# One set-up stage that also norms the memory, and head norms that take their roots of 12 rows

## The reference, cut to what matters

```python
def rms_norm(x, g):
    xf = x.astype(F32)
    y = xf * lax.rsqrt(jnp.mean(xf * xf, axis=-1, keepdims=True) + EPS)
    return (y * g.astype(F32)).astype(x.dtype)

def memory_attention(q_mem, mem, mem_norm_g, w_mem_kv):
    kv = rms_norm(mem, mem_norm_g) @ w_mem_kv
    ...

def diff_attention(q, k, v, lam, lam_init, subln_g):
    ...
    o = o.transpose(1, 0, 2, 3, 4).reshape(B, S, DA_HEADS, 2 * DA_HEAD_DIM)
    o = rms_norm(o, subln_g) * (1.0 - lam_init)
    ...

def hgrn2_mixer(h, mem, w_in, lb, out_norm_g, mem_norm_g, w_mem_kv, w_out):
    ...
    o = hgrn2_chunkwise(heads(q), heads(k), heads(i), heads(log_f))
    o = rms_norm(o, out_norm_g) * jax.nn.silu(heads(g).astype(F32))
    ...
```

## Time and profile before

| | us |
|---|---|
| median of 3 runs (3336.98 to 3337.41) | 3337.23 |
| the profiled execution | 3336.55 |
| its span from first to last instruction | 3334.8 |
| start of the first product of mem_kv | 41.99 |
| subln, from its first square to its last product | 182.18 to 197.83 |
| out_norm_b, likewise | 626.12 to 643.72 |
| first product of out_a, of out_b | 200.66, 646.52 |

### The profile page before, as it was taken

How to read it: one execution, slowest core, us unless ns; L and a number is a source line. 1 busy time by engine, 2 the same in 40 slices (tenths; PEclk the granted TensorE clock), 3 DMA queues, 4 the chain that set the end, 5 groups by cost and what they waited for, 6 DMA issues and landing times. The chain is left out here.

```text
span 3334.8 us, 41604 instructions
## 1 busy us (share of the span) xinstructions
PE 3026.1 (91%) x17165; PEld 2621.3 (79%) x17165; DVE 2031.3 (61%) x2255; ACT 1532.7 (46%) x1743; POOL 27.1 (1%) x47
## 2 busy tenths in 40 slices
PE   5979988679999999989999998999989896987898
PEld 5869876568888889678888887897788795985797
DVE  3547646545545457488898896545556565666645
ACT  3443343234434346367777775433334453432443
POOL 1001000000000000000000000000000000000000
PEclk9989998789999999999999999999999897988999
DMA  4428641034444546479999996533343341434042
GB/s 153 152 79 260 231 153 51 7 151 179 186 168 178 198 180 245 184 295 351 363 356 352 356 366 255 174 118 114 107 150 109 114 151 52 152 128 155 26 166 105
DMA packets 207408, 605.97 MB, mean 182 GB/s; under 512 B 20024, under 2 KB 78166, under 8 KB 163959
## 3 DMA queue, kind: packets, MB, share of 16 engines
q1 hardware_dynamic: 200906, 587.83, 48.5%
q0 software_dynamic: 4064, 12.75, 1.2%
q10 hardware_dynamic: 2253, 2.77, 0.3%
HBM read 602.26 MB, written 1.05 MB: 181 GB/s over the span
## 5 line engine op out<-in xcount | busy, mean ns | idle before, releaser
L1867 DVE TENSOR_TENSOR w_lo<-ring,w_hi 128x2048 fp32r<-128x2048 f32 x336 | 769.5, 2292 | 349.9 <-ACT w_hi L1769 345.0
L1769 ACT ACTIVATE w_hi<-ring 128x2048 fp32r<-128x2048 f32 x336 | 643.0, 1915 | 370.7 <-PE ps L1718 193.2
L344 DVE TENSOR_TENSOR w_lo<-ring,w_hi 128x2048 fp32r<-128x2048 f32 (+2 forms) x228 | 472.4, 2074 | 550.1 <-ACT w_hi L335 549.6
L335 ACT ACTIVATE w_hi<-ring 128x2048 fp32r<-128x2048 f32 (+2 forms) x228 | 396.4, 1739 | 709.7 <-PE ps L446 541.6
L446 PE MATMUL ps<-h_hi,w_hi 128*128 128x256 f32 x1608 | 462.4, 288 | 27.5 <-DVE w_lo L344 15.9
L446 PE MATMUL ps<-h_lo,w_hi 128*128 128x256 f32 x1608 | 459.0, 285 | 0.0
L446 PE MATMUL ps<-h_hi,w_lo 128*128 128x256 f32 x1608 | 458.9, 285 | 0.0
L446 PEld LDWEIGHTS ps<-h_hi,w_hi 128*128 128x128 f32 x1608 | 313.0, 195 | 31.9 <-issue 30.4
L446 PEld LDWEIGHTS ps<-h_lo,w_hi 128*128 128x128 f32 x1608 | 312.9, 195 | 0.2
L446 PEld LDWEIGHTS ps<-h_hi,w_lo 128*128 128x128 f32 x1608 | 312.8, 194 | 0.0
L1694 PE MATMUL ps<-w_hi,h_hi 128*128 128x512 f32 x448 | 179.4, 400 | 4.9 <-DVE w_lo L1867 4.9
(11 more groups left out here) (520 smaller groups left out, 6021.0 us busy)
## 6 DMA issues: line engine op xcount, KB each, us to landing
ring<-in_moe_w_gate_up SPq DMA_DIRECT2D x224, 1024.0 KB, 6.9
ring<-in_moe_w_down SPq DMA_DIRECT2D x112, 1024.0 KB, 6.8
ring<-in_w_in SPq DMA_DIRECT2D x54, 1024.0 KB, 6.9
ring<-in_w_in_even SPq DMA_DIRECT2D x28, 1024.0 KB, 7.0
ring<-in_dense_w_gate_up SPq DMA_DIRECT2D x22, 1024.0 KB, 7.7
ring<-in_w_in_odd SPq DMA_DIRECT2D x16, 1024.0 KB, 6.8
arena<-in_w_ada POOLq DMA_DIRECT2D x24, 512.0 KB, 5.0
ring<-in_w_out_even SPq DMA_DIRECT2D x12, 1024.0 KB, 7.3
```

Source lines behind the costliest of these rows:

```text
L335: k.nc.scalar.activation(self.part(k.w_hi, b, m), src, ACT.Copy).then_inc(k.hi_ready, 1)
L344: k.nc.vector.tensor_tensor(self.part(k.w_lo, b, m), src, self.part(k.w_hi, b, m).bitcast(F32), ALU.subtract).then_inc(k.lo_ready, 1)
L1769: nc.scalar.activation(high(g, h), raw(g, h), ACT.Copy).then_inc(k.hi_ready, 1)
L1867: nc.vector.tensor_tensor(low(g, h), raw(g, h), high(g, h).bitcast(F32), ALU.subtract).then_inc(k.lo_ready, 1)
```

## The change

`mem_norms` is gone as a stage; its work is written into `setup`, and so is the split of the first panel of mem_kv, which that stage then skips. The rows go out on three queues, 13 each (ACT, POOL and SP). SP loads `mem` and the identity first, then its rows, then `x` and the other constants, then the panels. ACT issues the four lambda vectors ahead of its rows. PE waits for rows and identity only. The mean of squares of the memory comes from `bn_stats` and `bn_aggr` on DVE in place of the sums on ACT. ACT and DVE hand over chunk by chunk, not in pairs.

subln and out_norm_b use a new function. Its 12 sums (6 heads by 2 tiles of tokens) are each put on a partition of their own by a matmul with a stationary operand of 12 columns, one of which is 1/128. Root and inverse are taken once, of 12x128 values. Twelve matmuls with a selecting operand then spread the inverses over 128 partitions in PSUM.

```diff
     def open_stage(self, prepare):
 
+        if self.at == 0:
+            return
         prepare(self.place(self.jobs[self.at][0], 0, 0), (1,) if self.begins_early(self.at) else (0, 1))
...
+def head_norm(k, name, x, gain, tmp, gate=None):
...
+        @st.block.scalar
+        def _(act):
+            nc.scalar.activation(k.stat[:, 0:1], k.eps(1e-6), ACT.Sqrt)
+            for p in range(pairs):
+                nc.scalar.activation(flat(tmp, p), flat(x, p), ACT.Square).then_inc(squared, 1)
+            act.wait_ge(sums_ready, 1)
+            nc.scalar.activation(root, k.ps[0:rows, 6, 0:P], ACT.Sqrt, bias=k.eps_cols[0:rows, 0:1]).then_inc(root_ready, 1)
+
+        @st.block.tensor
+        def _(pe):
+            pe.wait_ge(pick_ready, 1)
+            for h in range(HEADS1):
+                pe.wait_ge(squared, h // 2 + 1)
+                for t in range(TT):
+                    r = TT * h + t
+                    last = nc.tensor.matmul(k.ps[0:rows, 6, 0:P], pick[:, rows - 1 - r:2 * rows - 1 - r],
+                                            tmp[:, h, t * P:(t + 1) * P], start=(r == 0), stop=(r == rows - 1))
+            last.then_inc(sums_ready, 1)
+            pe.wait_ge(spread_ready, 1)
+            pe.wait_ge(scale_ready, 1)
+            for p in range(pairs):
+                for i in range(2 * TT):
+                    last = nc.tensor.matmul(k.ps[:, p, i * P:(i + 1) * P], spread[:, 2 * TT * p + i, :], root,
+                                            start=True, stop=True)
+                last.then_inc(scale_spread, 1)
+
+        @st.block.vector
+        def _(dve):
+            o = Order(dve, dve_order)
+            o(nc.vector.memset(pick, 0.0))
+            nc.vector.memset(pick[:, rows - 1:rows], 1.0 / P).then_inc(pick_ready, 1)
+            nc.vector.tensor_copy(spread, k.ident[0:rows, 0:rows].unsqueeze(2).broadcast_to([rows, rows, P])
+                                  ).then_inc(spread_ready, 1)
+            if gate is not None:
+                for p in range(pairs):
+                    dve.wait_ge(squared, p + 1)
+                    nc.vector.scalar_tensor_tensor(flat(x, p), flat(x, p), gain, flat(gate, p), ALU.mult,
+                                                   ALU.mult).then_inc(gated, 1)
+            dve.wait_ge(root_ready, 1)
+            nc.vector.reciprocal(root, root).then_inc(scale_ready, 1)
+            for p in range(pairs):
+                dve.wait_ge(scale_spread, p + 1)
+                if gate is not None:
+                    dve.wait_ge(gated, p + 1)
+                    nc.vector.tensor_tensor(flat(x, p), flat(x, p), k.ps[:, p, :], ALU.mult)
+                else:
+                    nc.vector.scalar_tensor_tensor(flat(x, p), flat(x, p), gain, k.ps[:, p, :], ALU.mult, ALU.mult)
...
         @st.block.sync
         def _(sp):
+            sp.dma_start(v.mem_tok, w["mem"].rearrange("(t p) d -> p t d", p=P)).then_inc(mem_loaded, 16)
+            sp.dma_start(k.ident[:, :], c["ident"]).then_inc(ident_loaded, 16)
+            sp.wait_ge(zeroed, 1)
+            for dst, src in pieces[2::3]:
+                sp.dma_start(dst, src).then_inc(rows_by_sp, 16)
             sp.dma_start(k.x[:, :, :], w["x"].rearrange("(t p) d -> p t d", p=P)).then_inc(loaded, 16)
-            sp.dma_start(v.mem_tok, w["mem"].rearrange("(t p) d -> p t d", p=P)).then_inc(loaded, 16)
             for dst, name in small:
                 sp.dma_start(dst[:, :], c[name]).then_inc(loaded, 16)
             k.stream.load_range(sp, 0, SLOTS)
...
         @st.block.scalar
         def _(act):
-            act.wait_ge(zeroed, 1)
-            for dst, src in pieces[0::2]:
-                act.dma_start(dst, src).then_inc(rows_loaded, 16)
             for i, name in enumerate(("a_lam_q1", "a_lam_k1", "a_lam_q2", "a_lam_k2")):
                 act.dma_start(lam[:, i, :], w[name].flatten().partition_broadcast(P)).then_inc(lam_loaded, 16)
+            act.wait_ge(zeroed, 1)
+            for dst, src in pieces[0::3]:
+                act.dma_start(dst, src).then_inc(rows_loaded, 16)
             act.wait_ge(lam_sums, 1)
             nc.scalar.activation(k.small[:, 2:4], k.small[:, 0:2], ACT.Exp).then_inc(lam_exps, 1)
+            act.wait_ge(mean_ready, 1)
+            nc.scalar.activation(k.stat[:, 4:6], k.stat[:, 2:4], ACT.Sqrt).then_inc(root_ready, 1)
+            act.wait_ge(columns_ready, 1)
+            for c in range(DC):
+                act.wait_ge(mem_turned, c + 1)
+                nc.scalar.activation(high_a[:, c, :], chunk(c), ACT.Identity, scale=gain_a(c)).then_inc(mem_high, 1)
+                nc.scalar.activation(high_b[:, c, :], chunk(c), ACT.Identity, scale=gain_b(c)).then_inc(mem_high, 1)
+            k.stream.round_weights(act, first_panel)
...
         @st.block.tensor
         def _(pe):
-            pe.wait_ge(rows_loaded, 16 * len(pieces[0::2]))
-            pe.wait_ge(more_rows_loaded, 16 * len(pieces[1::2]))
-            pe.wait_ge(loaded, 16 * (2 + len(small)))
+            pe.wait_ge(ident_loaded, 16)
+            pe.wait_ge(rows_by_sp, 16 * len(pieces[2::3]))
+            pe.wait_ge(rows_loaded, 16 * len(pieces[0::3]))
+            pe.wait_ge(more_rows_loaded, 16 * len(pieces[1::3]))
...
+            pe.wait_ge(mem_scaled, TT)
+            for c in range(DC):
+                if c == 6:
+                    pe.wait_ge(columns_ready, 1)
+                for t in range(TT):
+                    last = nc.tensor.transpose(chunk(c)[:, t * P:(t + 1) * P], k.xn[:, t, c * P:(c + 1) * P],
+                                               k.ident[:, :])
+                last.then_inc(mem_turned, 1)
...
         @st.block.vector
         def _(dve):
...
+            dve.wait_ge(mem_loaded, 16)
+            for t in range(TT):
+                for half in range(2):
+                    o(nc.vector.bn_stats(k.half_stats[:, t, half, :], v.mem_tok[:, t, half * 512:(half + 1) * 512]))
...
+            for c in range(DC):
+                dve.wait_ge(mem_high, 2 * c + 2)
+                nc.vector.scalar_tensor_tensor(low_a[:, c, :], chunk(c), gain_a(c), high_a[:, c, :].bitcast(F32),
+                                               ALU.mult, ALU.subtract)
+                nc.vector.scalar_tensor_tensor(low_b[:, c, :], chunk(c), gain_b(c), high_b[:, c, :].bitcast(F32),
+                                               ALU.mult, ALU.subtract)
+            k.stream.rest_of_weights(dve, first_panel)
```

More of the change, by code:

```diff
@@ L1017, in _ @@
                     nc.vector.tensor_tensor(of(out, p), of(tmp, p), of(gate, p), ALU.mult)
+def head_norm(k, name, x, gain, tmp, gate=None):
+    nc = k.nc
+    rows = HEADS1 * TT
+    pick = k.norm_row[:, 0:2 * rows - 1]
+    spread = k.norm_row[0:rows, P:P + rows * P].rearrange("p (r n) -> p r n", r=rows)
+    root = k.norm_row[0:rows, P + rows * P:2 * P + rows * P]
+    flat = lambda y, p: y[:, 2 * p:2 * p + 2, :].rearrange("p h n -> p (h n)")
+    pairs = HEADS1 // 2
+    with stage(k, name) as st:
+        dve_order, pick_ready, spread_ready = st.sem("dve_order"), st.sem("pick_ready"), st.sem("spread_ready")
+        squared, sums_ready, root_ready = st.sem("squared"), st.sem("sums_ready"), st.sem("root_ready")
+        scale_ready, scale_spread, gated = st.sem("scale_ready"), st.sem("scale_spread"), st.sem("gated")
+        @st.block.scalar
[43 more added lines that the diff above has]
+                    nc.vector.scalar_tensor_tensor(flat(x, p), flat(x, p), gain, k.ps[:, p, :], ALU.mult, ALU.mult)
@@ L2100, in setup @@
     nc = k.nc
-    small = [(k.ident, "ident"), (k.ones, "ones"), (k.upper, "upper"), (k.causal, "causal"),
+    small = [(k.ones, "ones"), (k.upper, "upper"), (k.causal, "causal"),
              (k.pair_rot, "pair_rot"), (k.half_rot, "half_rot"), (k.freq, "freq"), (k.cmp_mask, "cmp_mask"),
@@ L2142, in _ @@
             pool.wait_ge(zeroed, 1)
-            for dst, src in pieces[1::2]:
+            for dst, src in pieces[1::3]:
                 pool.dma_start(dst, src).then_inc(more_rows_loaded, 16)
@@ L2168, in _ @@
             nc.vector.memset(k.small[:, 4:5], 0.0).then_inc(lam_sums, 1)
+            dve.wait_ge(mem_loaded, 16)
+            for t in range(TT):
+                for half in range(2):
+                    o(nc.vector.bn_stats(k.half_stats[:, t, half, :], v.mem_tok[:, t, half * 512:(half + 1) * 512]))
+            for t in range(TT):
+                o(nc.vector.bn_aggr(k.moments[:, t, :], k.half_stats[:, t, :, :].rearrange("p h n -> p (h n)")))
+            mean, variance = k.moments[:, :, 0], k.moments[:, :, 1]
+            o(nc.vector.tensor_tensor(mean, mean, mean, ALU.mult))
+            nc.vector.scalar_tensor_tensor(k.stat[:, 2:4], mean, 1e-6, variance, ALU.add, ALU.add).then_inc(mean_ready, 1)
             dve.wait_ge(lam_exps, 1)
@@ L2375, in block1 @@
     attention(k, "diff_attention", groups + memory_groups(k, v.qm, v.km[0], v.vm[0], v.cat), v.work)
-    head_pairs = [((h, h + 2), WHOLE) for h in range(0, HEADS1, 2)]
```

(6 more changed lines are left out.)

43 lines of the change are left out of this document (28 added, 15 removed).

## The result

The changed kernel takes 3316.72 us (median of 4 executions, 3311.57 to 3319.36) against 3337.11 for the kernel before; the ratio is 0.9939, 95% interval 0.9927 to 0.9951. That is 20.4 us or 0.61% faster, clear of the 0.2%. The forecast was 3307.8 in a range of 3300.5 to 3314: right in direction, wrong in size by 9 us, and outside its range. The profiled execution took 3318.24 us, 18.3 less than that of before, where 29.4 were forecast.

What follows compares the result with a forecast made beforehand. PE was busy 91% of the span, but set-up (a DMA, PE, DVE, ACT chain) and two DVE-bound norms lay outside its cover. 14.9 + 14.5 = 29.4 us off 3336.55 gave 3307.2, with 0.7 for the median 3307.8; range 3300.5 to 3314.

Steps and rivals of the forecast that it cites:

- PE does four matmuls of 128 columns after each ... the first four spreading matmuls take 0.65 or 1.1: Norms: PE's sums after each square end at 3.9 us warm, 4.9 cold; first four spreading matmuls 0.65 or 1.1 us.
- the warm figure was 3.9: Norms: with PE at full clock the sums are there 3.9 us into the stage; cold, 4.9.
- The terms of 9.9 and 9.8 us: Cold lengths of the new norms: subln 15.65 - 9.9 = 5.7 us saved, out_norm_b 17.60 - 9.8 = 7.8.
- the 14.5 us of the two stages: Saving taken for subln and out_norm_b together, between 13.5 us cold and 16.7 warm.
- the cold transposes: Set-up's sixteen transposes in 3.30 us, read as PE's lower-clock pitch of 0.19 to 0.21 us a product.
- 1.16 for eight: Norms: eight matmuls in 1.16 us, read as a full-clock pitch of about 0.13 us for 128 columns.
- sums that may still be warm: Norms: the first sums of the squares may still meet the full clock, so 14.5 us saved was taken, cold being 13.5.
- The forecast of 8.3 warm: Norms: at full clock DVE paces the three last products and the stage ends at 8.3 us; cold, 9.9.
- Set-up: 14.9 forecast: First product of mem_kv moves from 41.99 to 27.1 us, saving 14.9; bounds 11.5 to 16.5.
- The lambda loads ... I take 8.0: Set-up: lambda loads, issued by ACT ahead of its rows, land by 7.5 to 11.6 us; 8.0 taken.
- The panel's wait: Rival: panels issued later become the wait; loss over 0.2% chance 0.02, milder delay eating set-up's gain (3322.7) 0.04.
- All later stages should keep their lengths: Sign to look for: stages behind the changed ones stay as long as before; wrong if one grows by what was won.

Runs made afterwards that it cites:

- one_record: The changed kernel with selecting operand and inverses as fp32r, so each spreading product rounds its inputs and is one record; 3309.34 us.
- squares_first: The changed kernel with one line moved: the root that only loads ACT's table comes behind the three squares in the norms; 3308.66 us.
- stats_first: The changed kernel with set-up reordered: DVE does the memory's statistics, root and scaling first, the lambda sums behind them; 3315.10 us.
- norms_only: The kernel before with only the new norms by head; set-up and memory norm as before; 3327.74 us.
- setup_only: The kernel before with only the merged set-up; both norms as before; 3322.92 us.
- later: The changed kernel plus two idle inversions of 12x128 behind the last product of out_norm_b, so out_b and router begin later; 3316.72 us.
- warm kernel: The changed kernel with PE multiplying constants into an unused bank where it would wait, around the norms and ahead of out_a and out_b; 3307.62 us.

## Why the forecast was wrong

- **The norms, the main fault.** The step "PE does four matmuls of 128 columns after each ... the first four spreading matmuls take 0.65 or 1.1" was mis-sized: it priced a record, and each of these fp32 products is two. In subln the sums ended 6.2 us into the stage and not 4.9, though only a part of them ran at the lower clock; in out_norm_b, at the full clock, they ended at 4.9 where the warm figure was 3.9. The spreading took 4.98 us and not some 2.8, which at 1.71 us a bank is above the 0.75 of DVE. The terms of 9.9 and 9.8 us measured 13.53 and 12.18, and the 14.5 us of the two stages 7.57. The earlier trace rows held the answer: 12 records for the six products that the code issues in each old norm. one_record shows it as the cause: at the full clock the spreading is 1.52 with single records and 2.91 with double ones.
- **A wrong reading that did no harm, by luck.** I took 0.19 to 0.21 us a product at the lower clock from "the cold transposes", but the window of those transposes shows the full clock, and a transpose is one record:

```profile
30.16:33.46 3.30, 3.30 (x16) 3.06 (x16) 0.55 (x2) 2.15 (x6) 0.00 (x0) 1.00 0.00 0
```

  A spreading record at the lower clock happens to take the same 0.21 us. The figure for the full clock, 0.13 from "1.16 for eight", should read 0.145; a spreading record took 0.12.
- **The clock in the norms.** I took the lower level for PE's work in the norms, less 1 us for sums that may still be warm, and put it down as given. It was right for the spreading, half right for the sums of subln (0.67) and wrong for those of out_norm_b (1.00); had these met the lower clock too, the miss would have been larger. squares_first shows that the level hung on a line that I had priced at its own 1.5 us: 4.75 us in subln. The forecast of 8.3 warm was for half the records; with all of them, warm, the stage is 8.79.
- **Set-up: 14.9 forecast, 12.96 measured.** Two steps. "The lambda loads ... I take 8.0" was 11.16, inside my bounds (11.6), and it stood at the head of DVE's list, so the memory's scaling ended at 18.05 and not 15.3; stats_first gets 1.46 back. Rows landed at 15.2, for 14.5 taken, at the 7.3 us that POOL's large transfer took before. The panel's wait did not come.
- **The sum of stages.** "All later stages should keep their lengths" was false: -2.18 us net, of which the router -3.10. It comes with the new norms alone (norms_only 16.85, setup_only 13.76) and is gone in later (13.75) with the same norms: a loss of clock, and no fixed cost of the change's code.
- **What held**: the direction; the inversion of 12x128 at 0.94; the broadcast copy at 0.94 (1.0 forecast), hidden; the gated products hidden, 2.08 us ended well before the inversion; no gain from moving the first panel's split (from the end of DVE's low parts to the first product 2.66 us, 2.71 before).

Together: 29.4 - 1.9 (set-up) - 6.9 (norms) - 2.2 (clock behind) = 18.4 us, the 18.3 of the profile.

What stays open is why the clock fell where it did behind the norms and ahead of them, as in the router and in diff_attention of the warm kernel; no run separates the shift in time from what PE had been doing. Filling PE's wait in set-up with products ahead of mem_kv wasn't tried: all eight PSUM banks are in use by other engines there.

## What to carry to other kernels

Before pricing a new product, divide the records of a like one in the trace by the products that the code issues: here that factor of two made PE the bound of a stage that DVE had bounded. Compare times of PE only at the same granted clock. Put work that another engine waits for ahead of table loads, and a wait for late inputs behind work whose inputs are there; the first cost more than its own 1.4 us, since the longer idling of PE went with a lower clock in every new norm that was traced, the second just the wait (1.46). When stages are shortened, expect unchanged stages behind them to move by some microseconds with the clock, and judge small edits by stage lengths and by several executions.

## What the runs showed of the hardware

- PE's granted clock can fall to 0.50, and stay there, while PE is busy without a gap. In the router of the kernel before it fell at 684.8, 2.7 us into products whose moving operand has 8 columns (PE had idled 2.0 us before them); in the changed kernel's router it stayed at 0.50 for the 10 us of all 48, with PE busy for 6.00 of 6.00 us. In the warm kernel it fell at 182.7, after 7.5 us without a pause, most of them on products with 12 columns or 12 rows in the stationary operand. That the narrow products are the reason is not shown. The group of the changed kernel's router:

```profile
L448 PE MATMUL ps<-w_hi,h_hi 128*128 128x8 f32 x16 | 5.6, 353 | 2.0 <-issue 2.0
```

- At a mean granted clock of 0.55 a spreading record of 128 columns took 0.21 us (4.98 for 24), at the full one 0.12 (2.91 for 24). The same products with fp32r operands were one record each and not two, of 0.13 us at the full clock (1.52 for 12).
- An inversion on DVE costs the same for 12 and for 128 partitions: 0.94 against 0.949 us for 128 columns.
- Four loads of 32 KB that ACT issued first of all, the first at 0.74 and the last at 2.16 us, were all there only at 11.16, after the megabyte of memory that SP issued at 0.74 (that one was there by 8.53 in stats_first).
